# Spatial gating of a transformer layer: prepared beneath its projection and finished at the projection's end

## The reference

```
def _spatial_gating(z_in, v_gain, w_s, b_s):
    z = gelu(z_in); u, v = z[..., :512], z[..., 512:]
    mu = mean(v, -1); var = mean((v - mu) ** 2, -1)
    vn = (v - mu) * rsqrt(var + EPS) * v_gain
    vc = vn.reshape(B, S // 128, 128, 8, 64)
    sv = einsum('gij,bnjgc->bnigc', w_s, vc) + b_s
    return u * sv
c_out = _spatial_gating(p[..., :1024], ...)
d_out = _neighbourhood_attention(q, k, v, rpb)
x = x + concatenate([c_out, d_out], -1) @ od_w_out
```

## Time and profile before

| | us |
|---|---|
| median of 3 runs | 3757.43 |
| lowest and highest of them | 3757.35 and 3762.9 |
| the profiled execution | 3758.37 |
| its span in the profile | 3756.6 |

### The profile page before, as it was taken

How to read it: one execution, slowest core, us unless ns; L and a number is a source line. 1 busy time by engine, 2 the same in 40 slices (tenths; PEclk the granted TensorE clock), 3 DMA queues, 4 the chain that set the end, 5 groups by cost and what they waited for, 6 DMA issues and landing times. The chain is left out here.

```text
span 3756.6 us, 51028 instructions
## 1 busy us (share of the span) xinstructions
PE 3352.6 (89%) x21218; PEld 2741.0 (73%) x21218; DVE 2068.7 (55%) x2806; ACT 923.0 (25%) x1566; POOL 457.8 (12%) x346
## 2 busy tenths in 40 slices
PE   6988899999489999899968887899989669999998
PEld 4777788878377887688748885687868558778786
DVE  4465544453364454589865654433355564678744
ACT  2035400110062233123254331122020361110104
POOL 1000111010002544100023530000020000000001
PEclk8999999999689999899989998999999889999998
DMA  2121122232302553232210002122322201222222
GB/s 104 58 65 46 46 89 90 84 107 90 71 1 100 193 180 137 73 127 98 79 41 3 3 3 90 68 90 93 109 69 90 93 1 67 90 90 91 83 97 71
DMA packets 209875, 298.62 MB, mean 79 GB/s; under 512 B 32786, under 2 KB 111262, under 8 KB 209534
## 3 DMA queue, kind: packets, MB, share of 16 engines
q1 hardware_dynamic: 209662, 295.59, 23.6%
HBM read 291.25 MB, written 4.32 MB: 79 GB/s over the span
## 5 line engine op out<-in xcount | busy, mean ns | idle before, releaser
L440 PE MATMUL bank<-h_hi_cut,ring_hi_cut 128*128 128x512 f32 x1960 | 775.8, 396 | 71.0 <-DVE ring_cut L550 32.4
L440 PE MATMUL bank<-h_hi_cut,ring_cut 128*128 128x512 f32 x1960 | 768.2, 392 | 0.0
L440 PE MATMUL bank<-h_cut,ring_hi_cut 128*128 128x512 f32 x1864 | 732.0, 393 | 0.0
L491 DVE CAST ring_hi_cut<-ring 128x4096 fp32r<-128x4096 f32 (+5 forms) x97 | 198.0, 2041 | 653.2 <-DMA ring<-in_ffn_w_gu 140.6
L440 PEld LDWEIGHTS bank<-h_hi_cut,ring_hi_cut 128*128 128x128 f32 x1960 | 371.2, 189 | 154.4 <-issue 43.1
L440 PEld LDWEIGHTS bank<-h_hi_cut,ring_cut 128*128 128x128 f32 x1960 | 371.1, 189 | 80.0
L440 PEld LDWEIGHTS bank<-h_cut,ring_hi_cut 128*128 128x128 f32 x1864 | 353.4, 190 | 76.1 <-issue 2.2
L493 DVE TENSOR_TENSOR ring_cut<-ring,ring_hi_cut 128x4096 fp32r<-128x4096 f32 (+5 forms) x97 | 380.6, 3924 | 7.8 <-issue 0.6
L440 PE MATMUL bank<-hidden_cut,ring_hi_cut 128*128 128x512 f32 x848 | 325.4, 396 | 0.0
L327 POOL TENSOR_TENSOR work<-work 128x512 f32<-128x512 f32 x42 | 63.0, 1500 | 1709.4 <-ACT work L311 1708.2
L440 PEld LDWEIGHTS bank<-hidden_cut,ring_hi_cut 128*128 128x128 f32 x848 | 160.2, 189 | 40.0 <-issue 1.2
(11 more groups left out here) (577 smaller groups left out, 5940.5 us busy)
## 6 DMA issues: line engine op xcount, KB each, us to landing
ring<-in_ffn_w_gu SPq DMA_DIRECT2D x44, 1024.0 KB, 6.6
ring<-in_w_in SPq DMA_DIRECT2D x21, 2048.0 KB, 7.7
ada_w<-in_ada_w SPq DMA_DIRECT2D x12, 2048.0 KB, 8.0
ring<-in_w_up SPq DMA_DIRECT2D x22, 1024.0 KB, 6.4
ring<-in_w_ff_in SPq DMA_DIRECT2D x8, 2048.0 KB, 8.5
ring<-in_w_ff_out SPq DMA_DIRECT2D x8, 2048.0 KB, 8.0
ring<-in_ffn_w_down SPq DMA_DIRECT2D x8, 1536.0 KB, 6.6
ring<-in_w_out SPq DMA_DIRECT2D x6, 2048.0 KB, 7.9
```

What stands on the lines that cost most here:

```text
L440: last = nc.tensor.matmul(to, lhs, rhs, start=st and q == 0, stop=sp_ and q == len(parts) - 1)
L491: dve.tensor_copy(high, whole)
```

## The change

The gating loses its own blocks. `project` gets three more hooks: `pe_tail` and `dve_tail` run on TensorE and VectorE after the last slab, `sp_end` on SP after `run_ahead`. `w_s` and `w_st` get memory of their own. SP loads `w_s`, `v_gain` and `colmask` when the projection's block begins, the bands of heads 0 to 3 between the two slabs of `od_out`, the others after both. TensorE turns `w_s` at the start of slab 3, in banks 6 and 7, and ScalarE copies it. The sum over `v` comes from the gelu's accumulator, the squares and their sums from ScalarE; VectorE subtracts the mean after slab 2's tiles and scales after slab 3's. Mixing, gating, the transposes back and the copies (two on VectorE, two on ScalarE) come at the end of the projection's block. Semaphores of other stages are shared for it. The band flips and all that follows are as before.

```diff
@@ project @@
                 take(n - 1, at_two=(lambda: cut_ahead(dve)) if cut_next else None)
                 if tail:
                     tail_on_dve(dve, DT - 1, tail)
+                if dve_tail:
+                    dve_tail(dve)
...
                     run_ahead(sp, g, last_use, sp_last)
+                    if sp_end:
+                        sp_end(sp, last_use)
 
                 @block.tensor
                 def _(pe):
                     over_slabs(pe, pe_slab)
+                    if pe_tail:
+                        pe_tail(pe)
...
-                w_s, w_st = (h_hi_f[:, c:c + 2, :].rearrange("p t (g q) -> p (t g) q", q=P) for c in (0, 2))
+                w_s, w_st = (sb(ctx, n_, [P, 8, P]) for n_ in ("w_s", "w_st"))
...
-                load_stage((w_s, a["od_w_s"].rearrange("g i j -> i g j")), (v_gain[:], bass.AP(tensor=a["od_v_gain"].tensor, offset=0, ap=[[0, P], [1, S]])))
...
+                last_slot = (g_od_in["s0"] + g_od_in["n"] - 1) % 2
+                early_heads = range(0, 4) if last_slot else range(5, 8)
...
+                    if j == 1:
+                        return act.activation(v_c[:, m, :], ps[:], ACT.Gelu_apprx_tanh, scale=r_col[:, m:m + 1], accum_out=mean[:, m:m + 1])
...
+                def words_here(sp, j):
+                    if j == 1:
+                        sp.dma_start(w_s[:], a["od_w_s"].rearrange("g i j -> i g j")).then_inc(mg["words"].sem, 16)
...
+                def late_bands(sp, last_use):
+                    last_use(last_slot)
+                    bands_of(sp, [hd for hd in range(8) if hd not in early_heads])
+
+                def turn_weights(pe, j):
+                    if j == 3:
+                        until(pe, "words", 1)
                         for g in range(8):
-                            last = nc.tensor.transpose(bank[g // 4][:, g % 4 * P:g % 4 * P + P], w_s[:, g, :], ident)
+                            last = nc.tensor.transpose(bank[6 + g // 4][:, g % 4 * P:g % 4 * P + P], w_s[:, g, :], ident)
...
+                def weights_taken(pe, j, m):
+                    if j == 3 and m >= 2:
+                        until(pe, "wt_took", m - 2)
+
+                def gating_on_act(act, j):
+                    if j == 3:
+                        for n in range(2):
+                            until(act, "wt", n)
+                            act.activation(w_st[:, 4 * n:4 * n + 4, :].rearrange("p g q -> p (g q)"), bank[6 + n][:], ACT.Copy).then_inc(mg["wt_took"].sem, 1)
                         for t in range(ST):
...
+                            until(act, "sub", t)
+                            act.activation(o_tok[:, t, :], v_c[:, t, :], ACT.Square, accum_out=var[:, t:t + 1])
+                        act.drain()
+                        act.activation(var[:], var[:], ACT.Sqrt, bias=eps[:, 0:1], scale=1.0 / S).then_inc(mg["root"].sem, 1)
...
+                def mix_and_turn(pe):
+                    pe.wait_ge(dve_took.sem, dve_took.done(7))
+                    for t in range(ST):
+                        until(pe, "vn", t)
+                        for g in range(8):
+                            last = nc.tensor.matmul(bank[4 + t][:, g * HD:(g + 1) * HD], w_st[:, g, :], v_c[:, t, g * HD:(g + 1) * HD], start=True, stop=True)
+                        last.then_inc(mg["mixed"].sem, 1)
+                    pe.wait_ge(act_took.sem, act_took.done(11))
+                    until(pe, "gated", ST - 1)
+                    for k in range(4):
...
```

More of the change, by code:

```diff
@@ L219, in build @@
                                           "u", "u_sb", "h", "h_sb", "y_out", "yc", "ysq", "var", "rstd", "yn", "turn", "out", "fin")}
+        mg = dict(words=mq["table"], root=mq["root"], wt=en["turned"], wt_took=mp["took"], sub=mx["centered"], vn=en["scaled"], mixed=mixed,
+                  gated=gated, turned=turned)
         with nc.Block() as block:
@@ new lines, in words_here, with bands_of @@
+                def words_here(sp, j):
+                    if j == 1:
+                        sp.dma_start(w_s[:], a["od_w_s"].rearrange("g i j -> i g j")).then_inc(mg["words"].sem, 16)
+                        sp.dma_start(v_gain[:], bass.AP(tensor=a["od_v_gain"].tensor, offset=0, ap=[[0, P], [1, S]])).then_inc(mg["words"].sem, 16)
+                        sp.dma_start(colmask[:], a["c_colmask"]).then_inc(bands_here.sem, 16)
+                def bands_of(sp, heads):
+                    for hd in heads:
+                        for r in range(2):
+                            sp.dma_start(band[64 - 64 * r:128 - 64 * r, hd, :].rearrange("p (a c) -> p a c", c=64),
+                                         bass.AP(tensor=grid_rows.tensor, offset=hd * 15 * 127 + (1 - r) * 127,
+                                                 ap=[[1, 64], [127, 14], [1, 64]])).then_inc(bands_here.sem, 16)
@@ L2721, in _ @@
[L2721 to L2732, removed]
+                                last.then_inc(mg["wt"].sem, 1)
@@ L2733, in _, with gating_on_dve @@
+                def gating_on_dve(dve, j):
+                    if j == 3:
+                        dve.wait_ge(act_took.sem, act_took.done(7))
                         dve.tensor_scalar(mean[:], mean[:], 1.0 / S, None, ALU.mult)
@@ L2735, in _ @@
                         for t in range(ST):
[L2736 to L2743, removed]
+                            dve.tensor_scalar(v_c[:, t, :], v_c[:, t, :], mean[:, t:t + 1], None, ALU.subtract).then_inc(mg["sub"].sem, 1)
+                    if j == 4:
+                        until(dve, "root", 0)
                         dve.reciprocal(var[:], var[:])
@@ new lines, in gate @@
+                def gate(dve):
+                    for t in range(ST):
+                        until(dve, "mixed", t)
+                        for g in range(8):
+                            c = slice(g * HD, (g + 1) * HD)
+                            last = dve.scalar_tensor_tensor(o_tok[:, t, c], bank[4 + t][:, c], vec("b_s", g), u_c[:, t, c], ALU.add, ALU.mult)
+                        last.then_inc(mg["gated"].sem, 1)
+                    for k in (1, 3):
+                        until(dve, "turned", k)
+                        dve.tensor_copy(mix[:, k, :], bank[k][:])
@@ L2762, in build @@
+                for name, n in dict(words=2, wt=2, wt_took=2, sub=ST, root=1, vn=ST, mixed=ST, gated=ST, turned=4).items():
+                    mg[name].advance(n)
             bands_here.advance(17)
```

67 lines of the change are left out of this document (24 added, 43 removed).

## The result

The changed kernel takes 3715.06 us, the median of 4 runs (3713.92 to 3716.2), against 3757.39 us (3756.26 to 3762.9) for the kernel before, run beside it on the same chip. The ratio is 0.9884, with a 95% interval of 0.9869 to 0.9899: 42.3 us less. The forecast was 3713.5, with a range of 3706 to 3719.

The account below looks back on a forecast made before the run. The bound was a 64.0 us chain from the projection's end to the first flip. Its gain, 64.0 - 16.7 (bands) - 1.1 (transposes) - 2.3 (clock) = 43.9 us, gave 3713.5 us, range 3706 to 3719.

Parts of the forecast that it names:

- bands last, clock down, flips slow: Main case after the projection: band loads, not gating, end the wait, and flips start at a lowered clock; chance 0.52.
- First flip at E + 16.7: After the projection's end (E), the second od_w_out slab and eight late band loads delay the first flip 16.7 us.
- The base of 64.0: Kernel before: 64.0 us from the projection's end to the first flip, one chain of loads, statistics, mixing, gating and transposes.
- Transposes in slab 3, 1.1 us: Eight transposes of w_s between TensorE's projection slabs lie on the path and end the projection 1.1 us later.
- Clock at the flips, 2.3 us (1.8 to 2.8): TensorE's pauses before the flips drop its clock, so the flips lose 2.3 us, with 0 as the other end.
- Rival 2: The clock stays up over the pause before the flips: gain 46.2 us, time 3711.2 us; chance 0.14.
- rival 3: The mixing itself drops the clock; gating ends later than the bands, gain 42.2 us, time 3715.2 us; chance 0.15.
- Preparation, price 0: Statistics, scaling and copies on VectorE and ScalarE hide under the projection at no cost; TensorE's transposes are priced separately.
- a later cut of slab 4: Sign of being wrong: VectorE cuts the projection's slab 4 later; preparation was priced at nothing for delays below 4 us.
- Gating chain, 12.9 to 14.6 us after E: After the projection's end (E): mixing, last gating group, transposes, last copy and block end take 12.9 to 14.6 us.
- E + 12.7: Lower bound for the late bands' landing, 12.7 us after the projection's end, from an issue rate of 1.05 us each.
- rival 1: Gating ends last, bands are hidden; flips start 12.9 to 14.6 us after projection, time 3707 to 3711.5 us; chance 0.14.

Follow-up runs that it names:

- all_late: The changed kernel with no band loaded early: all 16 band loads stand behind the second od_out slab; 3719.76 us, ratio 0.9898 to the kernel before.
- bands_first: The changed kernel with its eight late band loads issued ahead of the second od_out slab instead of behind it; 3706.79 us, ratio 0.9863 to the kernel before.
- keep_busy: The changed kernel plus six unused fp32 matmuls behind the gating's last transpose, filling TensorE's wait for the bands; 3707.6 us, ratio 0.9867 to the kernel before.
- loads_beneath: The kernel before with only its loads moved: small loads and half the bands under the projection, other bands at its end; 3741.61 us, ratio 0.9949.
- own_memory: The changed kernel with bands of heads 4 to 7 in separate memory, so all load beneath the projection; 3703.42 us, ratio 0.9854 to the kernel before.
- all_beneath: own_memory with mixing, gating and transposes back put under the projection's last slab, all four copies on VectorE; 3702.32 us, ratio 0.985 to the kernel before.
- loads_free: loads_beneath with the late bands in memory free beneath the projection, so no band is issued behind the slab; 3729.42 us, ratio 0.9923 to the kernel before.

## Why the prediction was right

The total was right, and so was the mechanism: bands last, clock down, flips slow. The terms of the sum were each off by about 0.2 us or less, and a shift of 0.75 us in which the change has no part came on top. Term by term:

- **First flip at E + 16.7** (7.8 for the slab and 8 x 1.11): measured 16.75. all_late confirms the price of a load behind the slab (1.06 us, by transfer or by issue), bands_first that the slab ahead of them matters. The base of 64.0 was 63.95.
- **Transposes in slab 3, 1.1 us:** from the last `q_d` tile to the last `k_d` tile it is now 22.67 us (932.74 - 910.07); that distance was 21.76 before, so 0.91. The last `k_d` tile came at 931.08 and comes 1.66 us later now; the other 0.75 stands already at the first loads of `od_w_in`, 819.61 now and 818.86 before, ahead of every instruction that the change adds or moves. It is a difference between two executions: in the other runs, alike up to there, this issue comes between 817.53 and 821.04. The rows, before and then after:

```profile
818.86 90.82 SPq L270 DMA_DIRECT2D ring<-in_od_w_in  x5
...
819.61 14.29 SPq L273 DMA_DIRECT2D ring<-in_od_w_in  x2
```

- **Clock at the flips, 2.3 us (1.8 to 2.8):** 14.35 - 12.27 = 2.08, and keep_busy removed it (12.29 us) by keeping TensorE at work through the wait. The size is less sure than the cause. I took it from the 3.65 us of transposes that stood right ahead of the flips before, "because" of which they ran at 1.00; but in loads_beneath the same transposes stood there and the flips lost 1.6 us, and in all_late they lost 3.0 (15.24 - 12.27). So 2.08, inside 1.8 to 2.8, is in part luck. Rival 2 falls. So does rival 3: the mixing ran in 7.25 us at 1.00 where I had 7.8. By the rule of the Trainium skill ("TensorE: Matmul & The Clock Gate", section "HAM oscillation — how this bites in real kernels"), a wait for DMA between bursts starts the next burst cold; the trace agrees, with a wait of 5.93 us and these 2.08 us.
- **Preparation, price 0:** right. VectorE's work before the cut of slab 4 ended within its wait for that load (7.07 us before, 6.35 now). One of my signs of being wrong did show, a later cut of slab 4, by 1.1 us beyond the shift; the wait took it in, and the last slab began on time. ScalarE needed 5.2 us where I allowed 9.
- **Gating chain, 12.9 to 14.6 us after E:** too long. It is 11.5 us to the last copy in the change, and own_memory has 11.84 to the first flip. The mixing was over at E + 7.1, not 7.8, the waits around the last gating group were 0.2 us instead of 0.5, and the transposes took 1.94 us, the low end of my 1.9 to 3.65. The error cost nothing, since the loads end the wait. In the forecast it made the pause 2 to 4 us, which is 5.93.
- **Sum:** 63.95 - 16.75 - 0.91 - 2.08 - 0.75 = 43.5 us at the end of the flips, against the forecast 43.9; without the shift of 0.75 it is 44.2. The spans differ by 43.6, so what follows gave back nothing. The median's gap to the forecast, 1.6 us, is of the order of the scatter between runs.

One bound rested on a wrong idea. For the bands I gave E + 12.7 as the least, "by the issue rate" of the earlier trace rows, 1.05 us each. But behind the slab the issues take 12.59 us for eight, so SP is held until E + 13.0, later than the gating chain. The block cannot end before that. Had the loads themselves landed sooner, as rival 1 supposed, the flips would by my estimate still have started at about E + 13.7 in this order of the queue (13.0, and 0.7 from the last issue to TensorE's start as in loads_beneath). That rival's lower end, E + 12.9, was nearly this by accident. loads_beneath is where the same gap in my theory put the first flip 13.0 us too early.

For rival 1, the Trainium skill ("DMA: Bandwidth & Descriptors", section "Why small descriptors are slow (HBM only)") charges 11 bus cycles for 8 of data for pieces of this size. The trace after disagrees with the sum that I made from it, as the one before did: 207 GB/s against the slab's 402 is 0.51 of the rate and not 8/11. all_late has 1.06 us for a load, where that rule gave 0.8. What else slows these pieces no run shows; by the kernel they start at any multiple of 4 bytes, one word further for each partition, and no run moves the start. The measurement decides; going by it was what put the forecast on E + 16.7.

## What to carry to other kernels

When loads are moved beneath a stage, look at what stands ahead of them on their queue and at what waits for the queue's issuing engine. Eight loads behind a 2 MB slab can cost in two ways: in their own landing, which ends the wait in the change, and in a block that can't end until they are issued, which does in loads_beneath. Putting them first (bands_first) or giving them memory that is free earlier (own_memory) brought 7 us at this place, and 8 and 12 us in the medians, of which the rest is unexplained. Work that TensorE has to run anyway gains little by moving under a stage that TensorE bounds (all_beneath, 1.9 us); moving loads and the other engines' work there is what pays.

## What the runs showed of the hardware that was not expected

- **Issuing slows behind a transfer under way.** The same eight loads took SP 7.47 us to issue ahead of the slab (bands_first) and 12.59, 12.61 and 12.27 us behind it (the change, keep_busy, loads_beneath). The slab costs this once: all_late issued sixteen behind it in 21.02 us, 1.05 us for each of the added eight.
- **The same light matmuls kept a clock but didn't raise it.** The 64 mixing matmuls ran in 7.25 us right behind the projection, at 1.00. In loads_free they took 13.89 us behind a pause of 13.66 us, and in the kernel before 13.88 us at 0.50.
- **The same run-up can end at either clock.** In the kernel before, loads_free and loads_beneath the same 64 mixing matmuls and 16 transposes stand ahead of the flips, with the same pauses behind each. The flips began at 1.00 in the first two and at 0.50 in the third, at a cost of 1.6 us.
- **The same code farther on takes a different time.** keep_busy differs from the change only by six matmuls, worth 2.06 us at the flips, and its median is 7.5 us lower. To place the rest, take the first of the four-slab loads of `ffn_w_gu`, about 1100 us, and the third group of flips, about 2950 us. These rows are from the change and then from keep_busy, with the stretch between the marks last (columns as in the earlier trace rows):

```profile
1101.56 23.40 SPq L284 DMA_DIRECT2D ring<-in_ffn_w_gu  x4
...
L1150 PE MATMUL bank<-h,squares x16: 539/539/951, 2958.3 to 2965.7; 128*128 128x448 f32 x16
...
1101.56:2958.30 1856.74, 1678.39 (x13433) 1373.72 (x13431) 1035.75 (x1402) 493.14 (x768) 358.73 (x265) 0.95 0.26 88
```

```profile
1097.63 23.39 SPq L284 DMA_DIRECT2D ring<-in_ffn_w_gu  x4
...
L1150 PE MATMUL bank<-h,squares x16: 539/539/954, 2950.5 to 2957.9; 128*128 128x448 f32 x16
...
1097.63:2950.50 1852.87, 1676.24 (x13432) 1372.32 (x13432) 1034.91 (x1402) 493.26 (x768) 356.88 (x265) 0.95 0.26 88
```

From the one mark to the other it is 1856.7 us in the change and 1852.9 in keep_busy: 3.9 us for identical code. The chip is not the reason: all_late ran on the same chip as keep_busy and has 1856.1 us there. A possible cause is that idle gaps fall differently against the clock once everything is shifted by a few microseconds, as in the flips of loads_beneath. TensorE's busy time between the marks, which the clock would lengthen, is 2.2 us longer in the change (1678.4 against 1676.2), so this could hold about half of the difference. No run here isolates it, and it stays open. It is why the experiments are read at their own place, and why a median's few microseconds say little about an edit in this kernel.
